# Experts 1 to 7: token rows fetched by indirect DMA and added back by an accumulating scatter, in place of one-hot matmuls

## The reference

```python
def moe_swiglu(xn, w_router, we_gate, we_up, we_down):
    logits = (xn @ w_router).astype(jnp.float32)
    top_v, top_i = lax.top_k(logits, TOP_K)          # TOP_K = 2
    top_w = jax.nn.softmax(top_v, axis=-1)
    gates = jnp.sum(jax.nn.one_hot(top_i, N_EXPERTS, dtype=jnp.float32) * top_w[..., None], axis=-2)
    y = jnp.zeros_like(xn)
    for e in range(N_EXPERTS):                       # 8; w: 1024x3584, 1024x3584, 3584x1024, float32
        y = y + gates[..., e:e + 1].astype(xn.dtype) * swiglu(xn, we_gate[e], we_up[e], we_down[e])
    return y
```

## Time and profile before

| | us |
|---|---|
| median of 3 runs (1632.02 to 1632.85) | 1632.37 |
| profiled execution | 1634.87 |
| its span, from first to last instruction | 1632.50 |
| PE busy in the span | 1520.1 |
| DVE busy | 1253.9 |
| ACT busy | 1063.7 |
| POOL busy | 5.7 |

### The profile page before, as it was taken

How to read it: one execution, slowest core, us unless ns; L and a number is a source line. 1 busy time by engine, 2 the same in 40 slices (tenths; PEclk the granted TensorE clock), 3 DMA queues, 4 the chain that set the end, 5 groups by cost and what they waited for, 6 DMA issues and landing times.

```text
span 1632.5 us, 23447 instructions
## 1 busy us (share of the span) xinstructions
PE 1520.1 (93%) x7766; PEld 1285.8 (79%) x7766; DVE 1253.9 (77%) x1584; ACT 1063.7 (65%) x1345; POOL 5.7 (0%) x54
## 2 busy tenths in 40 slices
PE   6999799999876789999999999999999999999995
PEld 5887799998665678878878887887887887887884
DVE  6957454454575679989979988988988998998994
ACT  5655444443463367778777877777777777776872
POOL 1000000000000000000000000000000000000000
PEclk9999899999988889999999999999999999999998
DMA  8454265554142249979979989998997997997991
GB/s 261 153 164 150 83 228 180 181 187 155 34 155 78 78 157 389 373 267 381 369 275 371 369 314 331 365 352 292 377 361 280 387 363 268 376 373 269 379 371 50
DMA packets 188681, 430.49 MB, mean 264 GB/s; under 512 B 8446, under 2 KB 20060, under 8 KB 188636
## 3 DMA queue, kind: packets, MB, share of 16 engines
q1 hardware_dynamic: 188636, 429.90, 73.8%
HBM read 428.82 MB, written 1.05 MB: 263 GB/s over the span
## 4 chain that ended last, share of the span: by engine, by line
PE 88%; DVE 6%; ACT 3%; issue 2%; DMA 0%; DVEq 0%; ACTq 0%; SPq 0%
PE bank L425 85%; DVE w_lo L1386 2%; PE bank L881 1%; PE bank L435 1%; DVE xT_lo L1428 1%; ACT L977 0%; ACT w_hi L977 0%; DVE h L1956 0%; PE bank L606 0%; ACT xr L1094 0%; ACT scr L1267 0%; DVE stat L1406 0%; DVE stat L1407 0%; DVE stat L1405 0%; DMA late<-in_mem_dram 0%
## 5 line engine op out<-in xcount | busy, mean ns | idle before, releaser
L1386 DVE TENSOR_TENSOR w_lo<-raw,w_hi 128x1024 fp32r<-128x1024 f32 (+1 forms) x832 | 962.3, 1197 | 195.6 <-ACT w_hi L977 182.5
L977 ACT ACTIVATE w_hi<-raw 128x1024 fp32r<-128x1024 f32 (+1 forms) x832 | 846.1, 1043 | 296.9 <-PE bank L425 296.0
L425 PE MATMUL bank<-w_hi,xT_hi 128*128 128x512 f32 (+4 forms) x1118 | 442.1, 395 | 32.9 <-DVE w_lo L1386 18.5
L425 PE MATMUL bank<-w_hi,xT_lo 128*128 128x512 f32 (+4 forms) x1118 | 434.1, 388 | 0.0
L425 PE MATMUL bank<-w_lo,xT_hi 128*128 128x512 f32 (+4 forms) x1118 | 434.0, 388 | 0.0
L425 PEld LDWEIGHTS bank<-w_hi,xT_hi 128*128 128x128 f32 x1118 | 214.5, 192 | 77.7 <-DVE w_lo L1386 16.4
L425 PEld LDWEIGHTS bank<-w_hi,xT_lo 128*128 128x128 f32 x1118 | 214.3, 192 | 41.8
L425 PEld LDWEIGHTS bank<-w_lo,xT_hi 128*128 128x128 f32 x1118 | 214.9, 192 | 38.3
L425 PE MATMUL bank<-w_hi,aT_hi 128*128 128x512 f32 x560 | 221.4, 395 | 3.9 <-DVE aT_lo L1685 2.5
L425 PE MATMUL bank<-w_lo,aT_hi 128*128 128x512 f32 x560 | 223.0, 398 | 0.0
L425 PE MATMUL bank<-w_hi,aT_lo 128*128 128x512 f32 x560 | 219.7, 392 | 0.0
(11 more groups left out here) (323 smaller groups left out, 878.3 us busy)
## 6 DMA issues: line engine op xcount, KB each, us to landing
raw<-in_we_gate_dram SPq DMA_DIRECT2D x112, 1024.0 KB, 7.4
raw<-in_we_up_dram SPq DMA_DIRECT2D x112, 1024.0 KB, 7.6
raw<-in_we_down_dram SPq DMA_DIRECT2D x112, 1024.0 KB, 6.6
raw<-in_w_gate_dram SPq DMA_DIRECT2D x14, 1024.0 KB, 5.1
raw<-in_w_up_dram SPq DMA_DIRECT2D x14, 1024.0 KB, 5.2
raw<-in_w_down_dram SPq DMA_DIRECT2D x14, 1024.0 KB, 4.8
raw<-in_w_in_dram SPq DMA_DIRECT2D x16, 768.0 KB, 4.9
raw<-in_w_out_dram SPq DMA_DIRECT2D x8, 1024.0 KB, 5.2
```

What stands on the lines that cost most here:

```text
L425: return pe.matmul(o, a, b, start=start, stop=stop, skip_group_check=True, **kw)
L977: act.activation(split_piece(w_hi, c, shape, half), raw_piece(c, shape, half), ACT.Copy).then_inc(hi_ready, 1)
L1386: dve.tensor_tensor(split_piece(w_lo, c, shape, half), raw_piece(c, shape, half), F(split_piece(w_hi, c, shape, half)), ALU.subtract).then ...
```

## The change

It touches experts 1 to 7 in what they read and experts 0 to 6 in what they add:

- POOL writes two tables to device memory ahead of the experts: `x_rows` (the normalised rows `xr`) and `h_rows` (`h`), 256 rows each and 128 spare rows of zeros. For slots without a token the index points to the spare rows.
- For each of units 1 to 7 an indirect DMA, issued by POOL, gathers 128 rows of 4 KB into `xg`, and PE turns them with 8 transposes in place of the 32 gather matmuls. Unit 0 keeps its gather by matmuls.
- For units 0 to 6 ACT writes the scaled result to `y_out` (two instructions, as `ys_hi` before), and an indirect DMA with addition scatters it into `h_rows`. `back`, `ys_lo` and the four additions of DVE remain for the last unit alone (and for the extra units). POOL copies `h_rows` back to `h` after the seventh scatter.
- The row indices come of the turn matmuls, now two columns wide (gate value and token number plus one); three small DVE instructions (`slots`) turn them into integers. `mark` for the next unit moves to the beginning of a unit, the turn matmuls to behind the first step, `slots` to where `mark` was.
- In unit 0, `slots(0)` stands between `gathered(0)` and the next low parts on DVE, and `keep_gate(0)` between `gathered(0)` and the next high parts on ACT.
- POOL's part is written out for each unit, with no loop. A one-column Silu ahead of the loop is added on ACT.

```diff
+            tokens = lambda rows: rows[0:S, :].rearrange("(b p) d -> p b d", p=P)
+            pool.wait_ge(sem("rows_normed"), 10)
+            pool.dma_start(tokens(x_rows), xr[:, :, :]).then_inc(sem("x_rows_here"), 16)
+            pool.dma_start(tokens(h_rows), h[:, :, :]).then_inc(sem("h_rows_here"), 16)
...
+            pool.wait_ge(sem("slots_known"), 1)
+            pool.tensor_copy(rows_now[:, :], rows_next[:, :]).then_inc(sem("slots_kept"), 1)
+            for u in range(NE - 1):
+                pool.wait_ge(sem("slots_known"), u + 2)
+                pool.wait_ge(sem("gather_psum"), 2 * u + 2)
+                pool.indirect_dma_start(xg[:, :], None, x_rows,
+                                        bass.IndirectOffsetOnAxis(ap=rows_next[:, 0:1], axis=0)).then_inc(
+                    sem("rows_gathered"), 16)
+                pool.wait_ge(sem("y_scaled"), 2 * u + 2)
+                pool.indirect_dma_start(h_rows, bass.IndirectOffsetOnAxis(ap=rows_now[:, 0:1], axis=0), y_out[:, :],
+                                        None, compute_op=ALU.add).then_inc(sem("scattered"), 16)
+                pool.wait_ge(sem("rows_gathered"), 16 * u + 16)
+                pool.wait_ge(sem("scattered"), 16 * u + 48)
+                pool.tensor_copy(rows_now[:, :], rows_next[:, :]).then_inc(sem("slots_kept"), 1)
+            pool.dma_start(h[:, :, :], tokens(h_rows)).then_inc(sem("h_back"), 16)
...
+            def turn_next(u):
+                pe.wait_ge(sem("onehot_ready"), u + 2)
+                pe.wait_ge(sem("turned"), u + 1)
+                pe.wait_ge(sem("slots_known"), u + 1)
+                turn(u + 1)
+            def gathered_turned(u):
+                pe.wait_ge(sem("rows_gathered"), 16 * u)
+                for k in range(KD):
+                    last = pe.transpose(B[k // 4][:, (k % 4) * P:(k % 4 + 1) * P], xg[:, k * P:(k + 1) * P], ident[:, :])
+                    if k % 4 == 3:
+                        last.then_inc(sem("gather_psum"), 1)
...
                 e_step(0, True)
+                if last:
+                    turn_rows()
+                else:
+                    turn_next(u)
                 with pe.Fori(1, NF - 1) as i:
                     e_step(i, False)
                 e_turn(n0 + NF - 1)
                 if not last:
-                    gather(u + 1)
+                    gathered_turned(u + 1)
                 e_down(C_MOE + 40, more, n0 + NF - 1, False, True)
-                if not last:
-                    pe.wait_ge(sem("gather_ready"), 2 * u + 4)
-                    e_in(C_MOE + FFN_CHUNKS, 0, more)
-                back(u)
-                if not last:
-                    turn(u + 1)
+                if last:
+                    back(u - (NE - 1))
+                    return
+                pe.wait_ge(sem("gather_ready"), 2 * u + 4)
+                e_in(C_MOE + FFN_CHUNKS, 0, more)
+                pe.wait_ge(sem("y_scaled"), 2 * u + 2)
...
+            act.activation(small[:, 63:64], iota[:, 0:1], ACT.Silu)
...
+            def keep_gate(u):
+                act.wait_ge(sem("slots_known"), u + 1)
+                act.activation(gslot[:, :], slot[:, 0:1], ACT.Copy).then_inc(sem("turned"), 1)
...
                 act.wait_ge(piece_used, 2 * (C_MOE + FFN_CHUNKS + more))
+                if not last:
+                    act.wait_ge(sem("scattered"), 16 * u + 32)
...
+                if not last:
+                    act.wait_ge(sem("y_scaled"), 2 * u + 2)
+                    keep_gate(u + 1)
             gathered(0)
+            keep_gate(0)
...
+            def slots(u):
+                dve.wait_ge(sem("turn_psum"), u + 1)
+                dve.tensor_copy(slot[:, :], B[3][:, S:S + 2]).then_inc(sem("slot_copied"), 1)
...
+                if not last:
+                    dve.wait_ge(sem("turn_psum"), u + 1)
+                    mark(u + 1)
...
                 if not last:
-                    mark(u + 1)
+                    dve.wait_ge(sem("slots_kept"), u + 1)
+                    slots(u + 1)
...
             gathered(0)
+            slots(0)
             for j in (4, 5):
                 split_low(2 * C_MOE + j, UP)
```

More of the change, by code:

```diff
@@ L176, in hybrid_trunk @@
             tab = sb("tab", [P, UNITS, 3, TB], scope=part)
-            cur = sb("cur", [P, 3, TB], scope=part)
+            cur = sb("cur", [P, 4, TB], scope=part)
             over = sb("over", [P, 8, NE], scope=part)
@@ L181, in hybrid_trunk @@
             gslot = sb("gslot", [P, 1], scope=part)
+            xg = sb("xg", [P, D], scope=part)
+            y_out = sb("y_out", [P, D], scope=part)
+            slot = sb("slot", [P, 2], scope=part)
+            no_token = sb("no_token", [P, 1], scope=part)
+            rows_next = sb("rows_next", [P, 1], I32, scope=part)
+            rows_now = sb("rows_now", [P, 1], I32, scope=part)
+        x_rows = nc.dram_tensor("x_rows", [S + P, D], F32, kind="Internal").ap()
+        h_rows = nc.dram_tensor("h_rows", [S + P, D], F32, kind="Internal").ap()
         flat = lambda t: t.rearrange("p a b c -> p (a b c)")
@@ L403, in _ @@
                       allow_small_or_imprecise_dtypes=True).then_inc(sem("ident_ready"), 1)
+            step(pool.iota(row_no[:, :], [[P, TB + 1]], base=1, channel_multiplier=1,
+                           allow_small_or_imprecise_dtypes=True))
             fill(upto[:, :, :], 1.0, [[0, 2], [1, P]], 0, -1, ALU.is_ge, 0.0)
@@ L894, in e_down, with back @@
                     last.then_inc(piece_used, 1)
-            def back(u):
-                pe.wait_ge(sem("ys_ready"), 2 * u + 2)
+            def back(v):
+                pe.wait_ge(sem("ys_ready"), 2 * v + 2)
+                pe.wait_ge(sem("onehotT_ready"), v + 1)
                 for t in range(TB):
@@ L901, in back @@
                         if t:
-                            pe.wait_ge(sem("h_added"), 4 * u + half + 1)
+                            pe.wait_ge(sem("h_added"), 4 * v + half + 1)
                         for n, ys in enumerate((ys_hi, ys_lo)):
@@ L1345, in unit @@
                         split_high(p0 + 2 * FFN_CHUNKS + j, UP, more, lap)
+                if last:
+                    act.wait_ge(sem("rows_turned"), u - (NE - 1) + 1)
+                    act.activation(onehotT[:, :], B[3][:, 0:S], ACT.Copy).then_inc(sem("onehotT_ready"), 1)
                 act.wait_ge(piece_used, 2 * (C_MOE + FFN_CHUNKS + more))
+                if not last:
+                    act.wait_ge(sem("scattered"), 16 * u + 32)
                 for half in range(2):
-                    act.activation(ys_hi[:, half * 512:(half + 1) * 512], B[4 + half][:, :], ACT.Copy,
-                                   scale=gslot[:, 0:1]).then_inc(sem("ys_hi"), 1)
+                    act.activation((ys_hi if last else y_out)[:, half * 512:(half + 1) * 512], B[4 + half][:, :], ACT.Copy,
+                                   scale=gslot[:, 0:1]).then_inc(sem("ys_hi" if last else "y_scaled"), 1)
+                if not last:
+                    act.wait_ge(sem("y_scaled"), 2 * u + 2)
+                    keep_gate(u + 1)
             gathered(0)
+            keep_gate(0)
             with act.Fori(0, NE - 1) as u:
@@ L1361, in _ @@
                     gathered(NE + j)
+                    act.wait_ge(sem("ys_hi"), 2 * j + 2)
+                    keep_gate(NE + j)
                     unit(NE + j, last=True)
@@ L2006, in unit @@
                 gathered(u + 1)
-                for j in (2, 3):
+                for j in range(2, 6):
                     split_low(p0 + 2 * FFN_CHUNKS + j, UP, more)
[L2009 to L2012, removed]
             gathered(0)
+            slots(0)
             for j in (4, 5):
@@ L2027, in _ @@
                     gathered(NE + j)
+                    dve.wait_ge(sem("slots_kept"), NE)
+                    slots(NE + j)
                     for i in (4, 5):
```

40 lines of the change are left out of this document (28 added, 12 removed).

## The result

The kernel after takes 1598.24 us (median of 4 runs, 1597.78 to 1600.07), the kernel before in the same comparison 1632.61 us: a ratio of 0.9752, 95% interval 0.9713 to 0.9791 (this is not the quotient of the two medians, which is 0.979; one of the four runs of the kernel before took 1644.39 us). The forecast was 1603.4 us, a gain of 29.0 us; the gain is 34.4 us by the medians and 37.1 us by the two profiled executions (1634.87 and 1597.78 us, spans 1632.5 and 1596.0 us).

What follows compares the result with a forecast made beforehand. PE was taken as the bound, with DVE and DMA a few per cent behind, so gains had to come at the seven changes of unit. −30.3 + 4.9 − 3.6 = −29.0 us gave 1603.4 us, range 1594 to 1621.

Steps and rivals of the forecast that it cites:

- seven changes of unit: PE's path from one expert to the next: 4.33 us saved at each, 30.3 us for seven.
- 56 slices: The experts' slices, 16.99 us each: taken as unchanged, with no term in the sum.
- unit 0: First expert: PE stands still 3.1 us ahead of the second e_in, plus one clock fall of 1.8: 4.9 us lost.
- clock, units 1 to 7: Clock falls behind the 1.92 us wait: four taken in place of six, 1.8 us each, 3.6 us won.
- The gather: Change of unit: 8 transposes replace 32 matmuls, then e_down waits for aT_lo; 1.98 us saved, not 2.88.
- Back and turn: Change of unit, between the two e_in: 3.10 us leave; turn matmuls behind the first slice cost 0.45 again.
- new wait of 0.3: Second e_in of a change: the second pair of pieces, behind the Silu, comes at 845.8, wanted at 845.5.
- DMA, POOL and DVE at nothing: Gather (8 us) and scatter hidden, extra traffic and DVE's changes cost zero; other ends 28.3 us (DMA), 6.3 us (DVE).
- rival 1: Gather comes late, PE stands before the transposes in all seven changes: slower, 1668 us; chance 0.07.
- rival 2: DMA becomes the bound through the added traffic, half of 28.3 us shows: 1617.6 us; chance 0.13.
- rival 3: DVE late, held up by each indirect DMA and the moved mark, PE waits: 1620.6 us; chance 0.08.
- Rival 4: Table loads stay, or the clock falls in every unit and twice in unit 0: 1612 us; chance 0.06.

Runs made afterwards that it cites:

- experiment 4: Kernel after with PE's 32 one-hot gather matmuls put back in units 1 to 7, the gathered rows left unused: 1622.83 us, ratio 0.9888.
- Experiment 1: Unused tile behind iota: 32 bytes a partition in the kernel before, 1626.45 us; in the kernel after, 32 bytes 1606.96 us, 64 bytes 1594.82 us.
- experiment 5: Kernel after with 15 useless transposes ahead of the turn matmuls of each of units 1 to 7: 1622.5 us, against 1599.68 us for the kernel after.
- experiment 3: Kernel after with unit 0's turn matmuls directly behind its gather, ahead of the first e_in: 1593.24 us, ratio 0.9723.
- experiment 6: Kernel after with three more indirect gathers of 0.5 MB behind each gather, into an unused tile: 1599.13 us, ratio 0.9737.
- pad_after: Kernel after with an unused tile of 32 bytes a partition behind iota: 1606.96 us, ratio 0.9799.

## Why the prediction was right and wrong

The sign, the steps of the change of unit and nearly every wait were right; the gain was forecast too small, because the 56 slices were put at nothing and the clock at four falls. By the terms of the sum, forecast and trace:

| term | forecast | measured | from |
|---|---|---|---|
| seven changes of unit | −30.3 | −29.0 | (25.87 − 21.18 − 0.43 − 0.12) × 7 |
| 56 slices | 0 | −6.7 | (16.56 − 16.44) × 56 |
| unit 0 | +4.9 | +6.4 | 37.78 − 31.34 |
| clock, units 1 to 7 | −3.6 | −9.7 | 6 × 1.61, six falls gone |
| ahead of the experts | 0 | +1.4 | gather of unit 0 at 573.85 and 572.43 |
| sum | −29.0 | −37.6 | spans −36.5 |

The measured sum is 1.1 us more than the spans have; that rest is not found.

- **Change of unit: right.** The gather was said to save 1.98 us and `e_down` to wait for `aT_lo`; the two traces have 1.87 (3.96 against 2.09 us from `e_turn` to `e_down`), and experiment 4 has 1.81. Back and turn were put at 3.10 − 0.45 − 0.3 = 2.35, and 2.88 − 0.43 − 0.12 = 2.33 is what is left for them (the 0.12 is the faster `e_down`, which the table counts with the slices). The turn matmuls behind the first slice cost 0.43 (76 matmuls in 16.87 us, 72 in 16.44). The new wait of 0.3 is 0.18 and stands where it was put, at the pieces behind the Silu. The total is 4.14 against 4.33.
- **The slices: the step that failed.** "From there on everything is as before" took a slice of 16.99 us as fixed, since its instructions are, and put this term at nothing; the low end of the range, 1594 us, has it at nothing too. It is the largest miss of the sum. The trace held a hint: the three products of `e_down`, matmuls of one shape, are spaced 0.23, 0.24 and 0.23 us there. A new tile of 12 bytes in each partition moved `aT`, and 0.12 us in each of 56 slices made 6.7 us. Experiment 1 shows that the place of the tiles alone does this.
- **The clock: sized wrong.** A fall behind the wait of 1.92 us costs 1.6 us (7.36 − 5.75), not 1.8, since the undisturbed row there takes 5.75 and not 5.50. The count matters more: "I take four in place of six" had no working. In units 1 to 7 of the trace none is left, and unit 0 has two, not one. Together the clock gave 9.7 − 3.5 = 6.2 us, where 3.6 − 1.8 = 1.8 had been taken. Experiments 4 and 5 show that 1.65 or 1.8 us more in a unit bring all seven back, which fits falls that went with the shorter unit; nothing in the trace of the kernel before tells that the new length would have none.
- **Unit 0: right in the wait, one clock fall short.** The wait of 3.1 is 3.3 us, where it was said to be, and experiment 3 takes it away. The second fall brings the unit to 6.4 us lost, a little over the stated 2 to 6.
- **DMA, POOL and DVE at nothing: right.** The gather was taken at 8 us and lands after 8.2; rivals 1, 2 and 3 fall, by the waits of the trace and by experiment 6. The Trainium skill, "DMA: Bandwidth & Descriptors", section "Anatomy of one DMA — SWDGE (gpsimd) path", gives about 2 us fixed and the bytes at 436 GB/s, an estimate of 3.2 us for 0.5 MB; beside full queues the trace has 8.2, so here it served only as a lower bound. The Trainium skill, "SBUF — State Buffer", section "SBUF: two separate sides", has GpSimd locked out of writing descriptors while DVE runs an instruction in a two-port mode; the trace shows no hold-up of either: POOL needs 1.78 us to issue 128 rows while DVE is busy 94% of the time, nearly all of it with `tensor_tensor`. An instruction of DVE in a two-port mode beside POOL's gather was not tried. The traffic of a unit was taken as 1.57 MB; the trace has 1.05 MB of it on POOL's queue.
- **Rival 4** is refuted in its first half by ACT's timeline, which has no table load in the lap. Of its second half the two falls in unit 0 came, and none of the falls in the other units.

What stays open: which distance of tiles slows `e_down`, why a unit of 123.0 us has no clock fall and one of 124.7 has seven, why executions of one kernel differ by up to 19 us, and why the start of the experts scatters by 6 us.

## What to carry to other kernels

When a change touches the list of tiles, the matmuls that it does not touch may still change: read the spacing of identical matmuls before and after, and try unused tiles of 32 and 64 bytes: one was worth 3 to 6 us of 1600 in three kernels here, and cost 9 in a fourth (pad_after). Where the clock falls in some laps of a loop and not in others, give its count a term of its own with both ends (none, all), because less than 2 us more in the lap brought all of them back here. And read what an engine's queue holds behind a wait: one product put two instructions later on DVE was worth 13 us, more than a third of what the whole change gained.

## What the runs showed of the hardware

- The place of tiles in SBUF changes the pace of fp32r matmuls: the same 72 take 16.36, 16.43, 16.44, 16.52 or 16.56 us, by the small tiles that lie ahead of the stationary operand of 24 of them, the only operand of the 72 that is moved.
- The TensorE clock falls from 2.4 to 1.2 GHz for a while behind the same idle time of 1.92 us in one kernel and not in another: in none of seven laps of 123.0 us, in all seven of 124.7 and 124.8 us. A fall costs 1.6 us, 24 matmuls in 7.35 in place of 5.75 us.
- An indirect DMA of 128 rows of 4 KB takes POOL 1.78 us to issue (the accumulating one 1.58) and lands after 8.2 us (7.7) beside full queues; three more in each lap (0.93 to 1.92 us to issue each, 7.5 us to land) cost nothing, and no low part of DVE took longer than 1.29 us, where their median is 1.22.
